# Feed-forward in half blocks: weight loads ahead of stores, rows finished one by one, sums and additions moved, the second memory split earlier

## The reference

```python
# first block, after attention
x = x + jnp.sum(gates * branches, axis=2) @ w_out[l]
h2 = rms_norm(x, norm_ffn[l])
x = x + (jax.nn.silu(h2 @ w_ffn_gate[l]) * (h2 @ w_ffn_up[l])) @ w_ffn_down[l]   # D_FF = 2816
...
# second block, first layer
z = h @ mla_w_in[j]
mem_kv = (mem @ w_mem_kv[layer]).reshape(b, MEM_LEN, 2, N_MEM_HEADS, HEAD_DIM)
```

## Time and profile before

| | us |
|---|---|
| median of three runs | 3265.19 |
| the profiled execution, its own time | 3261.54 |
| its span | 3259.7 |
| busy: TensorE, VectorE, ScalarE, GpSimd | 3104.6, 1740.3, 1332.9, 811.5 |
| mean granted TensorE clock | 0.984 of full speed |

### The profile page before, as it was taken

How to read it: one execution, slowest core, us unless ns; L and a number is a source line. 1 busy time by engine, 2 the same in 40 slices (tenths; PEclk the granted TensorE clock), 3 DMA queues, 4 the chain that set the end, 5 groups by cost and what they waited for, 6 DMA issues and landing times. The chain is left out here.

```text
span 3259.7 us, 50403 instructions
## 1 busy us (share of the span) xinstructions
PE 3104.6 (95%) x18600; PEld 2629.8 (81%) x18600; DVE 1740.3 (53%) x3480; ACT 1332.9 (41%) x2640; POOL 811.5 (25%) x994
## 2 busy tenths in 40 slices
PE   7999999999999999998898888998999999999999
PEld 7988889999998888886677677776987777687777
DVE  6567683433454133256555455796343566753776
ACT  5456564444453222133222222444343555622452
POOL 3424334344440000011333332160011110023131
PEclk9999999999999999999999999999999999999999
DMA  5010001111113121131222223743210000122012
GB/s 198 34 46 21 33 21 59 43 48 58 50 50 101 49 75 49 55 136 41 83 86 79 94 81 113 246 140 132 70 45 18 23 15 26 68 82 88 27 54 102
DMA packets 77412, 231.27 MB, mean 71 GB/s; under 512 B 17712, under 2 KB 21936, under 8 KB 65648
## 3 DMA queue, kind: packets, MB, share of 16 engines
q1 hardware_dynamic: 77168, 228.05, 19.8%
HBM read 183.92 MB, written 43.84 MB: 70 GB/s over the span
## 5 line engine op out<-in xcount | busy, mean ns | idle before, releaser
L2470 PE MATMUL ps<-whi,hhi 128*128 128x256 f32 (+2 forms) x1920 | 580.0, 302 | 2.2 <-ACT ig L2718 0.8
L2470 PE MATMUL ps<-whi,hlo 128*128 128x256 f32 (+2 forms) x1920 | 563.8, 294 | 0.0
L2470 PE MATMUL ps<-wlo,hhi 128*128 128x256 f32 (+2 forms) x1920 | 563.4, 293 | 0.0
L2470 PEld LDWEIGHTS ps<-whi,hhi 128*128 128x128 f32 x1920 | 368.1, 192 | 12.2 <-ACT ig L2718 1.8
L2470 PEld LDWEIGHTS ps<-wlo,hhi 128*128 128x128 f32 x1920 | 368.5, 192 | 7.3
L2470 PEld LDWEIGHTS ps<-whi,hlo 128*128 128x128 f32 x1920 | 367.9, 192 | 7.6
L2470 PE MATMUL ps<-hhi,whi 128*128 128x512 f32 x864 | 342.6, 397 | 0.0
L2470 PE MATMUL ps<-hhi,wlo 128*128 128x512 f32 x864 | 337.3, 390 | 0.0
L2470 PE MATMUL ps<-hlo,whi 128*128 128x512 f32 x864 | 336.6, 390 | 0.0
L3069 POOL CAST whi<-raw 128x512 fp32r<-128x512 f32 (+4 forms) x172 | 108.8, 632 | 651.1 <-PE ps L2470 641.7
L3080 POOL TENSOR_SCALAR stats<-stats 128x2 f32<-128x2 f32 (+2 forms) x230 | 60.1, 261 | 829.9 <-DVE stats L2841 353.4
(11 more groups left out here) (549 smaller groups left out, 7234.6 us busy)
## 6 DMA issues: line engine op xcount, KB each, us to landing
raw<-in_W SPq DMA_DIRECT2D x61, 1024.0 KB, 4.8
wf<-in_WF SPq DMA_DIRECT2D x22, 1024.0 KB, 4.8
scratch_fs<-fo SPq DMA_DIRECT2D x77, 256.0 KB, 2.0
raw<-in_W SPq DMA_DIRECT2D x24, 768.0 KB, 4.2
wd<-in_WD SPq DMA_DIRECT2D x44, 256.0 KB, 3.4
scratch_x<-x SPq DMA_DIRECT2D x16, 512.0 KB, 3.1
orw<-scratch_outs SPq DMA_DIRECT2D x6, 1024.0 KB, 5.6
xin<-in_x SPq DMA_DIRECT2D x8, 512.0 KB, 10.6
```

Of the source, the lines that this page charges most:

```text
L2470: x = e.matmul(r.out, a, b, start=(r.start and m == 0), stop=(r.stop and m == n - 1), skip_group_check=r.joined)
```

## The change

1. **Rows one by one.** Rows 4 to 7 each get both column halves in succession and are finished before the next (`by_row`). `first_weights(t)` spreads the sums and splits of set 0 over them. Set 1 is loaded and summed after the last of them. Both sets have places of their own for the first use (`wf0a`, `wf1a`) and for the rest (`wf0b`, `wf1b`). `norm_row` no longer turns the operand t3; `turn_t3` does it later.
2. **Strips 0 and 1.** Their pieces are in a new order; all the turns stand between them.
3. **Load ahead of the stores.** The load of strip i + 2 is called after p4 of strip i. Six of a pair's seven stores are called later, in `keep_sums`, at the end of the odd strip; those of the last pair in step 3 of the down stage.
4. **Last strip.** `prepare(0)` and `prepare(1)` each stand one piece later.
5. **Down sums.** The 44 `combine` calls of `prepare` go from GpSimd to VectorE.
6. **Additions.** `down_add` does at most two targets in a step, so the additions spread over up to eight steps.
7. **Next weights.** `w_split` goes to steps 52 and 63, and the loads to steps 56 and 67 in calls of their own.
8. **mem2.** The load is in step 69; the split is in halves, in steps 73 and 74; the `kv` products take PSUM banks that are not waiting for the last additions.

```diff
             for t0 in (0, 4):
+                if t0 and by_row:
+                    for t in range(4, 8):
+                        for j in range(2):
+                            p = DB.take()
+                            m = some(t, p, chunks[j](), numbered(t), len(blocks(t)))
+                            add(t, j, p)
+                            if j:
+                                pend.append(finish(t))
+                            tick()
+                        by_row(t)
...
-        def first_weights():
-            sets[1].sums(1)
-            sets[0].split(0, 0, 1, 2, 4)
-            sets[1].split(1, 0, 1)
-
-        for i in range(2):
-            sets[i].load(i)
-        sets[0].sums(0)
+        def first_weights(t):
+
+            if t == 4:
+                sets[0].sums(0)
+                sets[0].split(0, 0, 1, free=scr.free)
+            elif t < 7:
+                sets[0].split(0, *((4, 2) if t == 5 else (5,)), free=scr.free)
+
+        sets[0].load(0, raw_free)
         x_last = row_tiles(chunks, lambda t: views(hpair, sl(t * 128, 128)),
...
+        sets[1].load(1, x_last)
+        sets[1].sums(1, x_last)
...
-                fo_free[1] = [fs_store(1, k, fo_made[1]), sum4]
-                fo_free[3] = [fs_store(3, k, fo_made[3]), sum1]
-                fo_free[4] = [fs_store(4, k, sum1), sum2]
-                fo_free[2] = [fs_store(2, k, sum3)]
+                fo_free[2:] = [sum3], [sum1], [sum1, sum2], [sum2, sum4], [sum4]
                 fo_free[0] = fo_free[0] + [sum2]
-                fo_free[5] = [fs_store(5, k, sum2), sum4]
-                fo_free[6] = [fs_store(6, k, sum4)]
+                fo_free[1] = [sum4]
+                self.stored = [(1, fo_made[1]), (3, fo_made[3]), (4, sum1), (2, sum3), (5, sum2), (6, sum4)]
+
+            def keep_sums(self):
+                k = self.i // 2
+                for j, ready in self.stored:
+                    fo_free[j] = fo_free[j] + [fs_store(j, k, ready)]
...
         s0.p1()
+        s0.keep()
+        turn_t3(4)
+        turn_t3(5)
+        s0.p2()
...
             if kind == "t1":
-                made = combine(True, b.raw, at_("12"), at_("11"), ALU.subtract, got("12", "11"), b_free)
+                made = combine(False, b.raw, at_("12"), at_("11"), ALU.subtract, got("12", "11"), b_free)
...
             if more:
-                other.load(i + 1)
                 other.sums(i + 1)
...
             s.p4()
+            if i + 2 <= last_strip:
+                here.load(i + 2)
             s.c22()
             if more:
                 other.split(i + 1, 1, 2)
             else:
-                prepare(1)
+                prepare(0)
             s.p3()
             s.c21()
             if more:
                 other.split(i + 1, 4, 3)
+            else:
+                prepare(1)
             s.end()
+            if i % 2 and more:
+                s.keep_sums()
...
-            if before and k < 4:
-                down_add(p - 1, before, k)
+            if adds:
+                down_add(*adds.pop(0))
...
-            if s in (50, 56):
+            if i in (52, 63):
                 w_split()
-            if s == len(steps) - 6:
-                m2r = rest("m2r", [8, 256], F, m2_at)
+            if i in (56, 67):
+                w_load()
+            if i == 69:
                 t_m2 = load("mem2", m2r[:, :, :], d["mem2T"], t_split[3])
+            if i in (73, 74):
+                m2_free = t_split[7]
+                m2_lo = m2_split(i - 73)
...
-        emit("m2_split")
+        DB_ALL.i = (DB_ALL.i + 4) % 6
         for n in range(4):
-            down_add(6, before, n)
+            down_add(6, before, n, (1,))
```

More of the change, by code:

```diff
@@ L1446, in build, with __init__ @@
         class WeightSet:
-            def __init__(self, x, raw_at, sums_at, hi_at, raw_free_, sums_free, hi_free):
+            def __init__(self, x, raw_at, sums_at, hi_at):
                 self.x = x
[L1451 to L1468, removed]
+                self.first, self.then = [self.operands(f"wf{x}{n}", *a) for n, a in zip(("a", "b"), zip(raw_at, sums_at, hi_at))]
@@ L1469, in sums, with of, load @@
+            def of(self, i):
+                return self.first if i < 2 else self.then
+            def load(self, i, *free):
+                self.landed = load(f"wf{self.x}", self.of(i).raw4[:, :, :], d["WF"][i], *free, self.done[:4])
+            def sums(self, i, *free):
+                a11, a12, a21, a22, s1, s2, s4 = self.of(i).raw
+                sum1 = combine(True, s1, a21, a22, ALU.add, self.landed, self.done[4], *free)
                 sum3 = combine(True, a21, a11, a21, ALU.subtract)
-                sum2 = combine(True, s2, s1, a11, ALU.subtract, free[1])
@@ L1522, in norm_row @@
             hd_free[u % 2] = q.full
[L1523 to L1527, removed]
-            late_ops[u] = (two, four)
+            if t == 7:
+                turn_t3(7)
+            else:
+                p = row_T(late, t, r.scaled, [w[:, 4:8, :] for w in hpair])
+                h_read["b22"].append(p.read)
@@ new lines, in norm_row, with turn_t3 @@
+            two = combine(False, x0[:, early], x0[:, early], t3_of[t], ALU.add, row_full[u])
+            four = combine(False, x0[:, sl(512, 512)], x0[:, sl(512, 512)], x0[:, early], ALU.subtract)
+            late_ops[u] = (two, four)
+            if t == 7:
+                yield
+                p = row_T(late, t, r.scaled, [w[:, 4:8, :] for w in hpair])
+                h_read["b22"].append(p.read)
+            xsf_free[t % 2] = flat(p.full, two, three)
+        def turn_t3(t):
+            p = row_T(t3_of[t], t - 4, t3_made[t], (t3h, t3l), free=x_last)
+            h_read["t3"].append(p.read)
+            t3_full[t] = p.full
@@ L1657, in build @@
         tick()
-        fX_free[:] = [row_scaled[7], row_scaled[7]]
-        s0.keep()
+        turn_t3(6)
+        turn_t2(0)
+        tick()
+        s0.p5()
+        tick()
+        assert not pend
+        fX_free[:] = [row_scaled[7], row_scaled[7]]
+        fT_free[:] = [flat(xsf_free[0], t3_full[6]), flat(xsf_free[0], t3_full[6])]
+        turn_t2(1)
+        sets[0].split(0, 3, 6, free=x_last)
+        s0.p7()
+        turn_t2(2)
+        turn_t2(3)
+        sets[1].split(1, 0, 1, free=x_last)
@@ L1660, in build @@
         s1.p1()
         s1.keep()
[L1662 to L1671 removed]
+        t4_full = [turn_t4(u) for u in range(2)]
+        s0.gate_early()
+        s0.p6()
+        t4_full += [turn_t4(u) for u in range(2, 4)]
         for j in range(7):
@@ L1673, in build @@
             fo_free[j] = flat(h_read["t2"], h_read["t4"], t4_full, [x1_kept[t] for t in range(4)])
-        s0.gate_early()
-        s0.p7()
-        s0.p5()
-        s0.p6()
-        sets[1].split(1, 2, 4, 5)
-        s1.p7()
         s0.u3()
+        s0.c22()
+        s1.p2()
+        sets[1].split(1, 4, 2, free=x_last)
         s0.p4()
-        s0.c22()
         sets[0].load(2)
-        sets[1].split(1, 3, 6)
+        s0.c21()
         s0.p3()
+        s0.end()
         sets[0].sums(2)
-        s0.c21()
@@ L1688, in build @@
-        s0.end()
+        sets[1].split(1, 5, 3, 6, free=x_last)
         s1.gate_early()
         s1.p6()
+        s1.p7()
         s1.p5()
         s1.u3()
-        sets[0].split(2, 0, 5)
+        sets[0].split(2, 0)
+        sets[0].split(2, 5, free=sets[1].done[2])
         s1.p4()
+        sets[1].load(3)
         s1.c22()
-        sets[0].split(2, 1, 2)
-        s1.p3()
-        s1.c21()
-        sets[0].split(2, 4, 3)
+        for j, p in ((1, 0), (2, 0), (4, 1), (3, 3)):
+            if j == 2:
+                s1.p3()
+                s1.c21()
+            sets[0].split(2, j, free=sets[1].done[p] if j > 1 else s0.m4.full)
```

150 lines of the change are left out of this document (85 added, 65 removed).

## The result

| | us |
|---|---|
| before, median of four runs | 3263.57 (3258.33 to 3266.27) |
| changed, median of four runs | 3161.31 (3160.11 to 3163.45) |
| ratio, 95% interval | 0.9689 (0.9672 to 0.9706) |
| profiled execution, before and changed | 3261.54, 3161.36 |

The forecast was 3153 in a range of 3128 to 3190: right in direction and mechanism, 8 us too low. Measured against the profiled execution, 100.2 us went where the sum said 111.9.

What follows compares the result with a forecast made beforehand. TensorE, busy 95% of the span, bounds the kernel, leaving only idle and slow stretches to win. Strips 82.3, start 7.3, down 14.0 and second block 8.3 sum to 111.9 off 3261.54; plus 3.65 gives 3153, range 3128 to 3190.

Steps and rivals of the forecast that it cites:

- the residue: Strips: p3 0.44 us late in even strips, ten times, 4.4 us left, with no slow clock behind.
- the mean 7.7: Strips: mean price of one stall, 5.5 us of waiting plus 2.2 of slow clock; also the gain expected in strip 21.
- The four things expected to stay: Start: row 4's turn 2.3, last row's chain 2.4, set 1's splits 2.5, strip 1's p6 4.9 plus 2.2 slow clock.
- the last row's chain, 2.4: Start: the last row's scaling, difference and turn were expected to keep costing 2.4 us.
- waits in products five and six alone: Down stage: sign of being right, with the stage near 222 us and waits only in these two products.
- Its remainder: Down stage: 9.2 us of the 23.2 slack to stay, 5.7 in products five and six, 3.5 behind the last strip.
- the 7.0: Second block's start: TensorE's 7.0 us wait for the additions to x1 that free a bank, expected to go.
- The 1.3 for a faster clock: Second block's start: 1.3 us of clock gain on top of 7.0, making 8.3.
- Rival 1: Even strips: GpSimd and VectorE lock each other, second split 1.66 us instead of 0.69, +32, 3185; chance 0.18.
- Rival 2: Down stage: VectorE bounds it, 0.3 us more a step in products three to five, +10, 3163; chance 0.08.
- Rivals 3 and 4: Strips: 3, fo sums alone hold GpSimd, +73, 3226, chance 0.05; 4, both sets' sums late, +150, 3303, chance 0.03.
- that one number: Strips: p3 is on time if the weights' sums start by 8.96 us after the strip's start.

Runs made afterwards that it cites:

- the first experiment: The kernel before with only the load of strip i + 2 behind p4 and the six stores behind the odd strip's end: 3186.11 us, ratio 0.9762.
- the earlier split: The changed kernel with one split of set 1 (the operand of p6) placed before strip 0's last product: 3156.10 us, ratio 0.9673.

## Why the prediction was right, and where it was off

**Strips, 82.3 forecast, 78.6 measured.** The chain held at every link: the load's place on SyncE, its arrival, the fo sums as the next thing in front of the weights' sums, and the 7.36 us from there to p3 (now 1614.59 - 1607.15 = 7.44). Two experiments show it from both sides: edit 3 alone takes 74 us off, and half of the stores in front of the load put 23 back. The step that was off is the residue: 8.1 us stand over the bare 380.8, where 4.4 was allowed. It is ten waits (4.9 in all), 0.16 us before each that the profile does not count as idle, and 0.16 on each product behind. The prediction's own lines show the second item: it calls p3 "6.5 late", which is the idle time, where the two starts give 1675.77 - 1669.07 = 6.70. Eleven times this 0.16 is 1.8 of the 2.0 us that it left unexplained and kept nothing of. Strip 21's cost was 5.0 us (a wait of 3.3 and 1.7 of slow product, 2024.15 to 2028.60 us for 2.72), not the mean 7.7; edit 4 took 4.5.

**Start, 7.3 forecast, 3.0 measured, and not told from none:** with the old order a second execution took 112.8 us. The four things expected to stay all stayed. Row 4's turn waits 1.8 (forecast 2.3), set 1's split 2.6 (2.5), p6 of strip 1 4.9 with 2.5 of slow product behind (4.9 and 2.2). The failed term is "the last row's chain, 2.4": it is 3.7 + 0.8 of waits and 2.1 of slow product (from 1509.06 to 1513.84 us for 2.72 of work), 6.5. Half of the miss is GpSimd's sums beside VectorE's two differences, 2 x 0.95 us. The edit that gave set 1 a load of its own after the last row is also what put its sums there; the prediction followed the load and not what the sums meet on the other engine.

**Down, 14.0 forecast, 11.7 measured.** Undone one by one in the changed kernel, the edits bring: the stores moved out of the way 7.2, the spread additions 5.1 (some 4 by product), the weights' loads 2.3 (not told from none as a sum), the sums on VectorE -1.3, which is 13.3 for 11.7 together. Its sign "waits in products five and six alone" did not come. The forecast had the sums right at nothing, and was wrong to give spreading nothing. Its remainder was 9.2. Behind the last strip 2.7 us stay (forecast 3.5). Products 5 and 6 keep 1.9 and 4.7, close to the 2.4 and 5.3 counted on VectorE; of the 2.0 that `prepare`'s lead was to give back 1.1 came. Product 4 keeps 0.6. What it did not have is product 7, 2.3 us longer than with the sums on GpSimd: it counted the raw loads as gone from in front of others, and the one of step 67, which goes out late because VectorE's additions are late, makes `fa2r` late.

**Second block's start, 8.3 forecast, 6.7 measured.** The failed term is the 7.0: that wait is gone, but one for x of 1.2 us is new, against the prediction's sign that there would be none. The waits for turned rows (`hlo`) were there before and stay, 4.7 us and now 4.8. The 1.3 for a faster clock nearly came: TensorE is busy 15.91 us instead of 17.01 with the same 89 matmuls.

**The rivals.** Rival 1 would have needed the second split to take 1.66 us; it takes 0.69. Rival 2 wanted 0.3 us in each step of products 3 to 5, beyond what was counted; they keep 0.0, 0.6 and 1.9 us (2.4 counted), so it did not come. What is true in it is that VectorE bounds products 5 and 6, by 6.6 us; what the sums cost there they save in product 4. Rivals 3 and 4 have fallen with the first experiment. All four terms came out under the forecast, by 1.6 to 4.3 us: each had allowed too little for the waits that a new order brings with it.

## What to carry to other kernels

A queue that issues in order makes every load wait for whatever the stores ahead of it wait for; look for the wait's engine last, and first for what stands in front of the load. That holds for the loads one moves as well: this change freed one load and put another in front of an operand of product 7. Work from there to a time by which the first instruction of the chain must start, in us from the stage's beginning: that one number told which of two orders stalls, and by how much. Judge a move between GpSimd and VectorE product by product; the stage's sum moved by 1.3 us while its parts were +6.8 and -8.9 us.

## What had not been expected

- A split beside GpSimd's sums takes 1.64 us instead of 0.69, and GpSimd's own sum is little longer, 1.54 to 1.59 instead of 1.27; an addition with one operand in PSUM keeps its 0.69 or 1.42 for two.
- A wait of the same length is followed by a product at full clock in one place and at the 1.2 GHz level in another. Strips with the load behind three stores waited 2.0 to 2.6 us and paid no more; strip 21 waited 2.5 in the kernel with edit 3 alone and its product took 4.3 us for 2.7. In the start a wait of 2.1 for `fU` was followed by 4.45 us in the kernel before and by 2.85 with edit 3 alone, one of 2.6 for `wf1al` by 2.8 in the changed kernel, 4.3 with the earlier split and 5.3 with the additions in one step, whose start is the longest of all (115.2 us). What decides between them these runs don't show; it makes stretches with several short waits differ by up to 3 us from one execution to the next.
